# A one-layer decoder step: the merge of the branches moved into the experts stage

## What is computed

```
merged = gt[:,:,0]*br_gla + gt[:,:,1]*(od @ w_br_dil) + gt[:,:,2]*(om @ w_br_mem)   # gt = sigmoid(gates)
h  = x + merged @ w_out
n2 = rms_norm(h, ln2_g)
y  = h + peer(n2, peer_wq, peer_keys, peer_u, peer_v)

def peer(x):                                   # 8 heads, 128 keys, 16 picks
    qh = (x @ wq).reshape(T, 8, 2, 128)
    s  = einsum('thcd,hckd->thck', qh, keys)
    sv, si = top_k(s, 16)                      # in each half
    sc, pos = top_k(sv[:,:,0,:,None] + sv[:,:,1,None,:], 16)
    eidx = take(si0*128 + si1, pos); gw = softmax(sc)
    act  = gelu(einsum('td,thkd->thk', x, u_tab[eidx])) * gw
    return einsum('thk,thkd->td', act, v_tab[eidx])
```

## Time and profile before

| what | us |
|---|---|
| median of 3 runs (4648.75 to 4655.8) | 4648.9 |
| the profiled execution's own time | 4646.97 |
| its span, from the first to the last instruction | 4645.3 |
| TensorE busy | 4167.1 (90%) |
| VectorE busy | 2470.2 (53%) |
| ScalarE busy | 1744.6 (38%) |
| GpSimd busy | 1516.7 (33%) |

### The profile page before, as it was taken

How to read it: one execution, slowest core, us unless ns; L and a number is a source line. 1 busy time by engine, 2 the same in 40 slices (tenths; PEclk the granted TensorE clock), 3 DMA queues, 4 the chain that set the end, 5 groups by cost and what they waited for, 6 DMA issues and landing times.

```text
span 4645.3 us, 55356 instructions
## 1 busy us (share of the span) xinstructions
PE 4167.1 (90%) x18639; PEld 2496.4 (54%) x18639; DVE 2470.2 (53%) x5406; ACT 1744.6 (38%) x4663; POOL 1516.7 (33%) x1389
## 2 busy tenths in 40 slices
PE   7999999998687989899898898998998988988987
PEld 6888888887555764444444344444444444444431
DVE  2111111113843754477667666666676666666665
ACT  2111111113622654244444444444444444444443
POOL 0000000001624531044444444444444444444443
PEclk9999999998788999999999999999999999999999
DMA  8899899794697765599999999999999999999998
GB/s 288 274 323 325 295 319 321 257 300 166 199 349 247 222 184 186 180 424 427 427 427 423 426 421 417 425 422 421 420 419 421 425 417 423 423 416 419 420 418 368
DMA packets 319029, 1635.93 MB, mean 352 GB/s; under 512 B 44721, under 2 KB 87953, under 8 KB 176914
## 3 DMA queue, kind: packets, MB, share of 16 engines
q0 software_dynamic: 162640, 1160.06, 60.0%
q1 hardware_dynamic: 120506, 251.00, 15.9%
q10 hardware_dynamic: 35648, 222.04, 14.2%
HBM read 1547.06 MB, written 311.74 MB: 400 GB/s over the span
## 4 chain that ended last, share of the span: by engine, by line
DMA 30%; PE 18%; ACT 5%; issue 3%; DVE 1%; POOL 0%; DVEq 0%; POOLq 0%; ACTq 0%; PEldq 0%
DMA ex_rows<-scratch_uv,ex_E 30%; PE ex_ps_y L2937 14%; PE ex_ps_q L2885 3%; ACT ex_diag L2636 1%; ACT L2624 1%; ACT L2619 1%; ACT ex_w L2628 1%; ACT ex_gel L2624 1%; PE ex_ps_t L2847 1%; POOL ex_rows L2567 0%; PE ex_ps_y L2931 0%; ACT ex_ex L2619 0%; DVE ex_dots L2781 0%; PE ex_ps_s L2919 0%; DVE ex_rows L2781 0%
## 5 line engine op out<-in xcount | busy, mean ns | idle before, releaser
L2937 PE MATMUL ex_ps_y<-ex_rows,ex_diag 128*128 128x512 f32 (+1 forms) x4224 | 2022.9, 614 | 277.3 <-ACT ex_diag L2636 256.1
L2781 DVE CUSTOM_DVE_ANT_0 ex_rows<-ex_rows,ex_n2u 128x1024 f32<-128x1024 f32 x1056 | 1294.9, 1226 | 868.4 <-DMA ex_rows<-scratch_uv,ex_E 857.8
L2567 POOL DMA_INDIRECT ex_rows<-scratch_uv,ex_E x1056 | 1197.3, 1134 | 1539.3 <-PE ex_ps_y L2937 1395.2
L2937 PEld LDWEIGHTS ex_ps_y<-ex_rows,ex_diag 128*128 128x128 f32 (+1 forms) x4224 | 747.0, 190 | 1401.6 <-ACT ex_diag L2636 711.6
L417 PE MATMUL pj_ps<-pj_w_hi,pj_nT 128*128 128x470 f32 x3072 | 913.3, 377 | 6.2 <-DVE pj_w_lo L253 5.0
L2624 ACT ACTIVATE ex_gel<-ex_dots 128x1 f32<-128x1 f32 x1056 | 214.3, 203 | 1386.6 <-DVE ex_dots L2781 1385.9
L417 PEld LDWEIGHTS pj_ps<-pj_w_hi,pj_nT 128*128 128x128 f32 x3072 | 580.0, 189 | 88.3 <-issue 10.4
L417 PE MATMUL pj_ps<-pj_w_lo,pj_nT 128*128 128x470 f32 x1536 | 577.9, 376 | 0.0
L281 DVE COPY pj_zo<-pj_ps 128x470 f32<-128x470 f32 x96 | 61.4, 646 | 699.8 <-PE pj_ps L417 477.8
L2636 ACT ACTIVATE ex_diag<-ex_ident,ex_w 128x128 f32<-128x128 f32 x1024 | 411.1, 401 | 33.4
L281 ACT COPY pj_zo<-pj_ps 128x470 f32<-128x470 f32 x96 | 51.9, 553 | 804.4 <-PE pj_ps L417 412.5
(11 more groups left out here) (387 smaller groups left out, 3616.7 us busy)
## 6 DMA issues: line engine op xcount, KB each, us to landing
pj_w<-in_w_in POOLq DMA_DIRECT2D x24, 1880.0 KB, 17.7
scratch_z<-pj_zo SPq DMA_DIRECT2D x192, 235.0 KB, 11.1
scratch_uv<-in_peer_u ACTq DMA_DIRECT2D x8, 4096.0 KB, 25.0
scratch_uv<-in_peer_v ACTq DMA_DIRECT2D x8, 4096.0 KB, 42.2
scratch_uv<-in_peer_u ACTq DMA_DIRECT2D x4, 8192.0 KB, 42.0
scratch_uv<-in_peer_v ACTq DMA_DIRECT2D x4, 8192.0 KB, 73.1
out_dk_s<-in_cache_dil_k ACTq DMA_DIRECT2D x8, 4088.0 KB, 42.5
out_dv_s<-in_cache_dil_v ACTq DMA_DIRECT2D x8, 4088.0 KB, 54.7
```

What stands on the lines that cost most here:

```text
L2567: pool.indirect_dma_start(out=rows[:, p % SLOTS, :], out_offset=None, in_=d["uv"], in_offset=bass.IndirectOffsetOnAxis(ap=E[:, turn % 4, k ...
L2781: nc.vector.tensor_tensor_reduce(out=row, in0=row, in1=n2u[:, tile % 2], scale=1.0, scalar=0.0, op0=ALU.mult, op1=ALU.add, accum_out=dots[ ...
L2937: last = nc.tensor.matmul(y[0:n, 512 * c:512 * c + 512], diag[:, p % DIAGS, 0:n], rows[:, p % SLOTS, D + 512 * c:D + 512 * c + 512], start ...
```

## The change

The merge stage goes away; its work is done in experts. Tiles 0 and 1 are merged at the start of experts, tiles 2 to 8 in the turns 0 to 6, one a turn. Attend now loads the `lse` of all eight tiles, works out all group weights at once, and loads `ident` too. The multiplication by the group weights moves from GpSimd to VectorE. Merged tiles 0 and 1 stay on chip; tiles 2 to 8 still go through `scratch_h`. Gates, groups, the gla branch and the turned rows are single buffered.

To make room, the ring of gathered rows has FEW = 5 buffers for the first 120 picks, then 8, of which three lie in the space of the gates, the gla branch and the turned rows. The query weights are no longer held from the start: nine heads (turns 1 to 7, 9 and 10) come one at a time into two buffers of 1 MB, and after turn 6 five heads are loaded into the space of `wb` and `od`. The first transfers read 1024 bytes a row. The tiles ahead of `rows` now add up so that the gathered rows start at multiples of 512 bytes; before they started 256 bytes past one.

```diff
 def merge(nc, d):
-    early = experts_early(nc, d) ... (the whole stage, some 230 lines)
+    pass
...
-    SLOTS = 8
+    IN_TURNS = NT - 1
+    FEW, SLOTS = 5, 8
+    ALL_FROM = (IN_TURNS * K + K // 2) // FEW * FEW
+    STREAM = (1, 2, 3, 4, 5, 6, 7, 9, 10)
+    PRODUCT_AT = (5, 6, 8, 9, 10, 11, 13, 14)
...  sync: before the turns
+            for b in range(3):
+                load_gate(0, b)
+            load_gla(0)
+            load_x(0)
+            for g in range(2 * PH):
+                sp.dma_start(... d["peer_keys"][g // 2, g % 2]).then_inc(keys_in, 16)
+            (g2, iota, wq0)
+            load_groups(1); load_head(0); load_head(1)
+            (gates and gla of tile 1, groups of tile 2, load_head(2), gates and gla of tile 2,
+             load_head(3), each behind its wait on first or gated)
+            for turn in range(IN_TURNS):
+                tile = in_turn(turn)                       # turn + 2
+                if tile + 1 < TILES:
+                    load_groups(tile + 1)                  # waits a_t
+                if turn == 0:
+                    sp.wait_ge(h_used, 1); load_x(1)
+                if turn + 4 < len(STREAM):
+                    load_head(turn + 4)                    # waits q_done of the buffer's last user
+                for b in range(3):
+                    if tile + 1 < TILES:
+                        (waits first, then gated)
+                        load_gate(tile + 1, b)
+                sp.wait_ge(added, NPRD * (tile + 1))
+                sp.dma_start(d["h"][tokens(tile), :], a_gla[0:width(tile)]).then_inc(m_stored, 16)
+                if tile + 1 < TILES:
+                    sp.wait_ge(m_stored, 16 * (tile - 1))
+                    load_gla(tile + 1)
+            for head in range(3, PH - 1):
+                sp.dma_start(held_heads[...], wq_dram[:, :, head * 256:(head + 1) * 256]).then_inc(held_in[head - 3], 16)
+            sp.wait_ge(a_t, TILES)
+            sp.dma_start(od[...], wq_dram[:, :, (PH - 1) * 256:PH * 256]).then_inc(held_in[PH - 4], 16)
...  gpsimd
-                    if p >= SLOTS:
-                        pool.wait_ge(v_done, p - SLOTS + 1)
+                    if held_before(p) is not None:         # p - 5, later p - 8
+                        pool.wait_ge(v_done, held_before(p) + 1)
+                    elif p >= FEW:
+                        pool.wait_ge(m_stored, 16 * IN_TURNS)
...  scalar: in the turns
+                    if in_turn(turn) is not None:
+                        if k == 4:
+                            turned_branches(in_turn(turn))
+                        if k == 6:
+                            gate_values(in_turn(turn))     # sigmoid, 128x3072
...  vector: start, then the turns
+            first_gated(0)
+            for q in range(NPRD):
+                gated_part(0, q)
+            for part in range(3):
+                mixed(1, part)
+            first_gated(1)
             added_rows(0)
             squares(0)
             dve.wait_ge(consts_in, 48)
             normed_rows(0)
+            gated_part(1, 0)
+            (route(0); gated_part(1, 1); gated_part(1, 2); route(1); gated_part(1, 3); mixed(2))
...
+                    if k == 1 and turn and in_turn(turn - 1) is not None:
+                        gated_part(in_turn(turn - 1), 3)
+                    if tile is not None:
+                        if k == 8:
+                            first_gated(tile)
+                        if k in (9, 12, 14):
+                            gated_part(tile, (9, 12, 14).index(k))
+                        if k in (10, 11, 13) and tile + 1 < TILES:
+                            mixed(tile + 1, (10, 11, 13).index(k))
...  tensor: start, then the turns
+            turn_branches(0)
+            product(0, 0)
+            pe.wait_ge(keys_in, 16 * 2 * PH)
+            turn_keys(0)
+            turn_keys(1)
+            product(0, 1)
+            product(0, 2)
+            product(0, 3)
+            turn_merged(0)
+            for part in range(2 * KD):
+                out_product(0, part)
+            turn_branches(1)
+            product(1, 0)
+            (turn_rows(0), queries, scores of turns 0 to 2, products 1 to 3 of tile 1 between them)
...
+                    if tile is not None:
+                        if k == 2:
+                            turn_branches(tile)
+                        if k in PRODUCT_AT:
+                            q, half = divmod(PRODUCT_AT.index(k), 2)
+                            product(tile, q, (half,))      # two matmuls
...  queries
-                    if turn == 1:
-                        pe.wait_ge(wq_in, 16)
+                    if turn in STREAM:
+                        pe.wait_ge(head_in[STREAM.index(turn) % 2], 16 * (STREAM.index(turn) // 2 + 1))
+                    if STREAM[-1] < turn < 2 * PH:
+                        pe.wait_ge(held_in[head - 3], 16)
```

More of the change, by code:

```diff
@@ L2808, in _ @@
             normed_rows(0)
-            for turn in range(2):
-                for part in range(K):
-                    route(turn, part)
+            gated_part(1, 0)
+            for part in range(K):
+                route(0, part)
+            gated_part(1, 1)
+            gated_part(1, 2)
+            for part in range(K):
+                route(1, part)
+            gated_part(1, 3)
+            for part in range(3):
+                mixed(2, part)
             for turn in range(TURNS):
+                tile = in_turn(turn)
                 for k in range(K):
```

551 lines of the change are left out of this document (258 added, 293 removed).

## The result

The changed kernel takes 4655.55 us (median of 20 runs), the kernel before 4648.29 us (20 runs beside them): ratio 1.0015, 95% interval 1.0008 to 1.0021. It is 7 us slower, by more than the measurement is uncertain. One of its 20 runs took 18,959 us and is left out of the ratio. The forecast was 4634 us and faster; the range, 4606 to 4682, holds the time. The profiled execution has a span of 4650.6 us, 5.3 us more than before.

What follows compares the result with a forecast made beforehand. The prediction took the experts as bound by DMA bytes, with no gathers for 191 us during the merge. First gather -112, ring start +7, bytes +78 and TensorE +12 made -15 us, hence 4634 us, range 4606 to 4682.

Steps and rivals of the forecast that it cites:

- First gather: Start of the experts: with the merge mostly moved under the gathers, the first gather comes at 1859.4 us, 112 us earlier.
- Start of the ring: First dots: gatings and a mix on VectorE come first, five buffers are full by then, 7 us lost to gathers.
- Bytes: Gather stretch of the experts: 30.1 MB moved under full DMA engines cost 2.6 us/MB, 78 us.
- Rival 2: Loads under the gathers: bytes cost the upper price, 95 us instead of 78, so no change, 4651 us; chance 0.18.
- The queries' waits on each head fall a turn or more after the load: Query weights in the experts' turns: each head is loaded a turn or more before the queries wait for it.
- TensorE under the gathers: Merging turns: TensorE's 47.8 to 52.2 us a turn against up to 51.9 of bytes loses 12 us.
- The ring's "1.7 us of slack": Five-buffer ring: a buffer's round of 10.7 us fits into 12.4 us of transfers, leaving 1.7 us.
- Sigmoid: ScalarE at k = 6: sigmoid with table loads costs nothing under other transfers; 3.6 us a turn without that cover.
- Rival 1: Merging turns: five buffers don't cover sigmoid, exponents and held VectorE, 6.9 us a turn, 4682 us, half of it 4658; chance 0.31.
- The gla chain: Merging turns: gating 3, store, gla load and first gating at k = 8 take 18 of 23 us, holding by 5.
- rival 4: Gathered rows: the 512-byte start matters, all gathers go at 427 GB/s, 31 us less, 4603 us; chance 0.04.
- rival 3: Whole change: all overlaps, 71 us for bytes, nothing for TensorE or ring start, -41 us, 4608 us; chance 0.11.

Runs made afterwards that it cites:

- e5: Kernel before with seven buffers and 52 extra loads (27.3 MB) from far-apart rows of z in tile 0: 4714.39 us, ratio 1.0149.
- e6: Kernel before with seven buffers and 52 extra loads (27.3 MB) from adjoining rows of x in tile 0: 4713.85 us, ratio 1.0145.
- e1: Changed kernel with tile 2's loads put ahead of three of the held heads on SyncE's queue: 4646.02 us, 0.9994 of the kernel before.
- e11: Changed kernel with tile 2's loads ahead of three held heads, and one matmul instead of four per branch product for tiles 2 to 8: 4623.80 us.
- e17: Kernel before with seven buffers, 52 extra loads in tile 0 and 16 extra matmuls in each of turns 0 to 6: 4719.74 us, ratio 1.0137.
- e18: Kernel before with five buffers, 52 extra loads in tile 0 and 16 extra matmuls in each of turns 0 to 6: 4913.72 us, ratio 1.056.
- e7: Kernel before with five gather buffers instead of eight throughout the experts, nothing else: 4857.75 us, ratio 1.0444.
- e9: Kernel before with five gather buffers throughout and 52 extra loads (27.3 MB) from z in tile 0: 4890.82 us, ratio 1.0532.
- e10: Changed kernel with tile 2's loads ahead of three held heads, and no sigmoid for tiles 2 to 8: 4642.59 us, 0.9991 of the kernel before.
- e3: Changed kernel with the gathered rows moved back to 256 bytes past a multiple of 512: 4651.59 us, 1.001 of the kernel before.
- e4: Kernel before with its gathered rows moved to start at multiples of 512 bytes: 4647.31 us, ratio 0.9999.

## Why the prediction was wrong, by its steps

- **First gather, -112 us: right, a little small.** 1859.4 was predicted, 1851.91 measured: -119.7, 7.7 us better, beyond the "up to 116" of the text. The last key load landed at 1792.6 us and not at 1798. (The sum ahead of that, redone, gives 1812.1 and not 1812.3 us for the last gating; that changes nothing.)
- **Start of the ring, +7 us: right.** 15.8 us from first gather to first dot against 8.3; "some 15" was said.
- **Bytes, +78 us: right.** 2.46 us/MB (e5, e6) against the 2.6 taken; 30.1 MB make 74 us. The packets between the first dot and turn 9 carry 31.9 MB more than before, which would be 78, so the 74 is good to a few us. Rival 2's upper price of 95 us fell, and where the rows lie doesn't matter.
- **"The queries' waits on each head fall a turn or more after the load": true, and beside the point.** This is the first step that failed. The heads came in time; what came late was the load behind them on SyncE's queue. I costed the held heads as bytes and not as issue time, and never named the merged rows of tile 2 that stand behind them. Measured: 16.1 us between two dots; 12.5 us at the start of turn 9 and some 10 us of the total come back in e1.
- **TensorE under the gathers, +12 us: the second step that failed, by a wait put at nothing.** 47.8 and 52.2 us a turn were sums of records without gaps, compared with 51.9 us of bytes, and the greater of the two was taken. TensorE's work was sized right, 50.0 us on the mean of turns 1 to 6 against 50.05 measured. What the step left out is that TensorE stands for diagonals meanwhile, 3.1 us a turn, 18.7 in these six. The prediction's figures make some 51 us a turn there; 53.2 were measured. The excess of turns 0 to 8 is 116.9 us; without the 12.5 us of the queue and 74 us of bytes 30 us are left where 12 stood. e11 takes back 18 us (e11 against e1) by cutting three quarters of the branch matmuls, so most of the 30 hangs on TensorE; e17 shows that TensorE's work alone doesn't cost it. "The greater of two" nearly held in e17 and e18 (49.0 and 49.7 us), where only TensorE had more to do; in the changed kernel three engines have blocks in the same round.
- **The ring's "1.7 us of slack": wrong by itself, right in its place.** The term that failed is the landing of a gather, 5.7 us taken from a gather alone, 8.4 on the mean with five in flight (e7); dot, weight, diagonal, sum and reissue take 5.1 there, as against the 5.0 of the text. So the round is 13.5 us and not 10.7, longer than 12.4, and gathers alone lose 3.6 us a turn. Beside other loads five buffers cost nothing (e9), as the text said, or 0.8 us with TensorE full (e18).
- **Sigmoid, 0: no gain from taking it out, but not free.** e10 takes the 5.3 us block away and gains 1 us over e1, within the intervals. Yet the traces have TensorE standing 9.9 us behind it in turns 1 to 6, and in e10 8.2 us behind VectorE's wait for the groups in its place: one wait covered the other. Rival 1's 3.6 us a turn for the sigmoid fell. Its account as a whole, blocks one after another that five buffers don't cover, is close to what the traces show, and the time lies near the 4658 us of half of it. No run gives the changed kernel more than five buffers, so how much of the 18.7 us the ring itself owes is not known.
- **The gla chain, "holds by 5 us": held.** VectorE waited for gla twice, 1.5 us in all. It waited three times, 6.7 us in all, for groups and memory branch, a load to which I gave no deadline.
- **The 256-byte shift, 0: right** (e3, e4); rival 4 fell.
- **What would show it.** A DMA share of 1.0 in turns 0 to 4 was to prove the account; it came, at 398 to 404 GB/s. The sign was in the rate. Tile 0's picks took 417.7 us, not 394. The 422 GB/s of the later turns came as predicted. The range began at 4606, two below rival 3's own 4608.

In sum, from turn 9's start: -15 - 7.7 (first gather) + 0.5 (ring start) + 12.5 (queue) - 4 (bytes) + 18 (TensorE and the chains around it) = +4.3 against +4.6 measured. The last term is what is left of turns 0 to 8, 30 us less the 12 predicted, so the sum closes by construction; that e11's gain is 18 us too is chance. By turns, 53.2 us against some 51 in turns 1 to 6 make 13 us of it, and TensorE's waits there are 18.7. How these waits divide between the sigmoid, VectorE's loads and the ring no run settles.

## What to carry to other kernels

When loads are moved ahead of others on one queue, cost their issue as well as their bytes, and write down what stands behind them: behind two transfers of 1,024 rows that were still on their way each further issue was held for 17 to 23 us, and four heads as one transfer of 1,024 wide rows went out in 0.43 us. When work is moved under a full DMA stretch, don't take the greater of two engines' sums; look for where each engine will stand for another, since with a short ring every in-order block (turning, queries, a sigmoid, a gating that waits for a load) falls into the same round. Take the landing of a gather from a trace with as many in flight as there will be. Judge a DMA-bound stretch by its GB/s, not by its busy share alone.
